# Block order at the end of an expert stage: the last up product ahead of the other block's down product

## The chip, the core and the metric

The kernel runs on one core of one Trainium2 chip. The metric is the device time of one execution in microseconds (us); the table below gives the median of three. The core's engines run side by side, each with its own list of instructions: TensorE (PE in the profile; its weight loads are PEld), VectorE (DVE), ScalarE (ACT), GpSimd (POOL) and SyncE (SP), which here only issues transfers. They wait for each other by semaphores.

## The reference, cut to what matters

The whole is a first block (norm, attention, a recurrent and a convolution branch, a mixture of experts) and a second block of two layers (a gated linear attention beside latent attention, then an FFT and gating mixer), on 1024 tokens of 1024 channels in fp32. The change lies where the experts end and the first layer of the second block begins:

```python
def run_block(args):                       # one expert, a block of its tokens
    xe, e = args
    return (jax.nn.silu(xe @ w_gate[e]) * (xe @ w_up[e])) @ w_down[e]
...
y = jnp.zeros((n_tok + 1, d), yb.dtype).at[slot_tok].add(yb * slot_gate[:, None])
...
# second block, layer 0: latents x and context ctx are normed and modulated, then projected
h_lat = modulate(x, shift, scale)
h_ctx = modulate(ctx, shift_c, scale_c)    # layer_norm(ctx) * (1 + scale_c) + shift_c
y_lat, y_ctx = even_mixer(h_lat, h_ctx, ...)
```

There are 32 experts; `w_gate` and `w_up` are 1024x512 for each, `w_down` 512x1024. The context has 256 rows and doesn't depend on the experts; the latents x do.

## The kernel before, in words

**Blocks of the expert stage.** The 32 experts are worked off in `NMB` = 26 blocks, numbered 0 to 25. Twenty are single experts with up to 128 tokens; six are pairs of two lightly used experts with up to 64 tokens each. Block 25 is a single one, block 24, ahead of it, is a pair. A block goes through: rows of its tokens gathered (POOL), turned on PE (`turn_tensor`), gate product (`product_tensor(p, n, 0, ...)`, "gu" n 0), up product ("gu" n 1), SiLU on ACT (L2162), hidden product silu(gate)*up on DVE ("hd", L2223), hidden rows turned on PE (`turn_hidden_tensor`, L2086) and copied (ACT L2173 or, for a pair, L2170, and DVE L2235), down product (`down_tensor`, two PSUM banks), output copies on ACT (`down_scalar`, L2181) and a scatter to `y2d` in memory by POOL (L2001).

**Weights.** Each of the three weights of a block comes as pieces of 1 MB: two of a single block, four of a pair. SP fetches them (L320) in the order of the list `turns`, into a ring of ten slots; a fetch waits until PE has done with what lay in its slot. The number before `_in` in a semaphore's name (`slot112_in`) is the slot. The weights of a single block are multiplied in three passes from a high and a low part: `WE.split_scalar` (ACT L385, two instructions for a piece) copies the rounded high part, `WE.split_vector` (DVE L394, two instructions) subtracts it. A product waits for the low part (`lo_done`). A pair's weights are used whole, without a split. ACT and DVE split three pieces ahead of the one in use (`ahead_scalar`, `ahead_vector`).

**Order.** The order on each engine is written out by hand: `experts_tensor`, `experts_scalar` and `experts_vector` loop over the blocks e: up product of e (with the rows of e+1 turned in its middle), gate product of e+1 (with the hidden rows of e turned in its middle), down product of e. In the last turn, without a block e+1, PE turns the hidden rows of block 25 and then the first half of the context (`nC.turn_tensor`, L527) ahead of block 25's down product.

**The context's norm.** ACT loads a table (L2471) and computes the reciprocal deviation (`stats_scalar`, L271 and L272); DVE makes the bias from it (`center_vector`, L491); ACT normalises one half of the rows (`norm_scalar`, L512), DVE the other (`norm_vector`, L500). Then PE turns them, and after block 25's output ACT (L553, L555) and DVE (L561, L574) scale and split them.

**What comes behind.** SP fetches two pieces of the next layer's weights: one once "gu" 25 1 is done, one once half of down 25 is done. POOL waits for "gu" 25 1, moves four tiles of x (`moves_pool`, L2385) and scatters block 25. When both last scatters have landed, SP loads `y2d` (L2378) and DVE combines the experts' outputs with x (`combine_vector`, L2394), from which the latents' norm and the next layer start.

## Time and profile before

| | us |
|---|---|
| median of 3 runs (lowest to highest) | 2316.39 (2315.34 to 2318.12) |
| the profiled execution | 2316.22 |
| its span, first to last instruction | 2314.4 |
| PE busy | 2163.4 (93%) |
| DVE busy | 1353.3 (58%) |
| ACT busy | 1030.2 (45%) |
| POOL busy | 365.9 (16%) |

The mean granted clock of TensorE was 0.979 of its full 2.4 GHz. Times in rows are counted from the span's start. The expert stage lies between about 600 and 1145 us, the place of the change between 1095 and 1160. In it the 16 DMA engines are busy over most of the time with the experts' weights, and PE nearly all of it; how the two end is what the rows below show.

### The profile page before, as it was taken

The page shows a single profiled execution, that of the slowest core. Times are in us where ns is not written, and L with a number is a line of the kernel's source. Part 1 is how long each engine was busy: PE and PEld are TensorE (multiplying, and loading weights), DVE is VectorE, ACT ScalarE, POOL GpSimd, SP SyncE. Part 2 cuts the span into 40 slices and gives each one's busy share as a digit, 9 for nine tenths or more (in the row PEclk, how much of TensorE's full clock was granted, in tenths as well). Part 3 has the DMA queues.
Part 4 walks back from the last instruction along what each step waited for, and adds up shares of the span by engine and source line. Part 5 has one row for each costly group of instructions (what it writes and reads, how often), then busy time and mean ns, then how long its engine had stood idle before and what let it go on. Part 6 is the DMA issues. An engine that isn't in the chain of part 4 may idle for free.

```text
span 2314.4 us, 26522 instructions
## 1 busy us (share of the span) xinstructions
PE 2163.4 (93%) x10595; PEld 1547.1 (67%) x10595; DVE 1353.3 (58%) x1733; ACT 1030.2 (45%) x1515; POOL 365.9 (16%) x263
## 2 busy tenths in 40 slices
PE   7999999898799998999879999988999999999998
PEld 6877755674676566565568777744555567788886
DVE  5787277456877457465572255566555556643385
ACT  4265366511666456455562234354544523402231
POOL 2000012000211011110200000013555623000014
PEclk9999999998999999999989999999999999999999
DMA  4111030217999999999661101030010031211041
GB/s 129 63 47 37 28 128 29 73 67 303 412 408 421 420 409 389 413 401 396 254 208 37 49 19 37 33 111 1 1 37 19 1 146 73 76 43 49 24 176 64
DMA packets 105889, 348.78 MB, mean 151 GB/s; under 512 B 21960, under 2 KB 54737, under 8 KB 79776
## 3 DMA queue, kind: packets, MB, share of 16 engines
q1 hardware_dynamic: 95040, 321.70, 36.3%
q0 software_dynamic: 9504, 21.08, 2.4%
q10 hardware_dynamic: 1216, 4.24, 0.5%
q8 instruction: 86, 1.41, 0.3%
q14 instruction: 43, 0.35, 0.0%
HBM read 323.21 MB, written 34.26 MB: 154 GB/s over the span
## 4 chain that ended last, share of the span: by engine, by line
PE 76%; DVE 9%; DMA 8%; ACT 5%; issue 2%; SPq 0%; POOL 0%; DVEq 0%; ACTq 0%; POOLq 0%
PE psm L236 72%; DMA mem<-in_exp_w_up_dram 4%; DVE small L3521 2%; DMA mem<-in_ada_w_dram 2%; DMA mem<-in_exp_w_gate_dram 1%; PE psm L1173 1%; ACT mem L1255 1%; DMA mem<-in_exp_w_down_dram 1%; PE psm L2040 1%; PE psm L527 1%; DVE r L350 1%; DVE r L394 1%; ACT r L385 1%; DVE mem L3226 0%; ACT mem L1209 0%
## 5 line engine op out<-in xcount | busy, mean ns | idle before, releaser
L236 PE MATMUL psm<-r,r 128*128 128x512 f32 (+3 forms) x6449 | 1544.9, 396 | 71.5 <-DVE r L2206 14.1
L236 PEld LDWEIGHTS psm<-r,r 128*128 128x128 f32 (+2 forms) x6449 | 1191.4, 190 | 408.4 <-issue 88.2
L236 PE MATMUL psm<-mem 128*64 128x512 f32 (+11 forms) x2870 | 464.0, 448 | 20.8 <-DMA mem<-in_ada_w_dram 10.7
L394 DVE TENSOR_TENSOR r<-mem,r 128x1024 fp32r<-128x1024 f32 x240 | 283.3, 1225 | 163.2 <-ACT r L385 160.4
L236 PEld LDWEIGHTS psm<-mem 128*64 128x64 f32 (+5 forms) x2870 | 205.3, 152 | 218.1 <-issue 160.7
L385 ACT ACTIVATE r<-mem 128x1024 fp32r<-128x1024 f32 x240 | 240.0, 1054 | 102.5 <-DMA mem<-in_exp_w_gate_dram 44.3
L3735 POOL TENSOR_TENSOR mem<-mem 128x1024 f32<-128x1024 f32 x63 | 152.5, 2421 | 161.7 <-ACT mem L3687 106.9
L3687 ACT ACTIVATE mem<-psm 128x512 f32<-128x512 f32 x160 | 94.4, 595 | 141.9 <-PE psm L236 135.3
L3521 DVE TENSOR_REDUCE small<-psm 128x1 f32<-128x1280 f32 x64 | 95.2, 1488 | 86.3 <-PE psm L236 86.3
L350 DVE TENSOR_TENSOR r<-mem,r 128x1024 fp32r<-128x1024 f32 (+2 forms) x72 | 76.9, 1111 | 79.8 <-ACT r L341 79.5
L1303 DVE TENSOR_TENSOR_SCAN mem<-mem,small 128x128 f32<-128x128 f32 (+7 forms) x64 | 83.7, 1356 | 24.3 <-POOL mem L1319 20.1
L271 ACT ACTIVATE small<-small 128x1 f32<-128x1 f32 (+2 forms) x34 | 10.0, 294 | 194.7 <-DVE small L431 123.9
L3876 POOL TENSOR_TENSOR mem<-mem 128x1024 f32<-128x1024 f32 (+1 forms) x15 | 35.7, 2379 | 375.5 <-ACT mem L3842 375.5
L236 PE MATMUL psm<-mem,cst 128*128 128x512 f32 (+4 forms) x222 | 79.4, 592 | 1.7 <-ACT mem L2685 1.0
L341 ACT ACTIVATE r<-mem 128x1024 fp32r<-128x1024 f32 (+2 forms) x72 | 63.2, 930 | 33.4 <-DMA mem<-in_w_in_dram 23.1
L1043 DVE SCALAR_TENSOR_TENSOR mem<-mem,small 128x1024 f32<-128x1024 f32 x60 | 76.9, 1281 | 1.3
L4058 ACT ACTIVATE mem<-psm 128x512 f32<-128x512 f32 x24 | 14.4, 598 | 138.3 <-PE psm L236 138.3
L2001 POOL DMA_INDIRECT y2d<-mem,small x26 | 27.1, 1042 | 304.1 <-ACT mem L2181 223.3
L1992 POOL DMA_INDIRECT mem<-h2d,small x26 | 31.0, 1193 | 209.5 <-DVE mem L2223 173.1
L574 DVE TENSOR_TENSOR r<-psm,r 128x256 fp32r<-128x256 f32 (+1 forms) x56 | 26.5, 492 | 47.8 <-ACT r L555 47.7
L1255 ACT ACTIVATE mem<-psm 128x1024 f32<-128x1024 f32 (+3 forms) x48 | 37.2, 811 | 38.0 <-PE psm L236 37.7
L1173 PE MATMUL psm<-cst,mem 128*128 128x128 f32 x288 | 42.5, 284 | 10.4 <-ACT mem L1209 9.6
(374 smaller groups left out, 1741.7 us busy)
## 6 DMA issues: line engine op xcount, KB each, us to landing
mem<-in_exp_w_gate_dram SPq DMA_DIRECT2D x64, 1024.0 KB, 17.4
mem<-in_exp_w_up_dram SPq DMA_DIRECT2D x64, 1024.0 KB, 17.4
mem<-in_exp_w_down_dram SPq DMA_DIRECT2D x64, 1024.0 KB, 17.8
mem<-in_ada_w_dram SPq DMA_DIRECT2D x32, 768.0 KB, 13.6
mem<-in_odd_w_in_dram SPq DMA_DIRECT2D x10, 1024.0 KB, 5.6
mem<-in_x_dram SPq DMA_DIRECT2D x16, 512.0 KB, 6.5
mem<-in_w_in_dram SPq DMA_DIRECT2D x8, 1024.0 KB, 5.3
mem<-y2d SPq DMA_DIRECT2D x8, 1024.0 KB, 7.0
```

The costliest lines, as they stand in the source:

```text
L236: return p.e.matmul(o, l, r, start=start, stop=stop, skip_group_check=True)
L341: p.e.activation(h, mem(self.raw(i), [R * n])[:, w * q:w * q + w], ACT.Copy).then_inc(*self.hi_done.up(i, q))
L350: p.e.tensor_tensor(l, mem(self.raw(i), [R * n])[:, w * q:w * q + w], h.bitcast(F32), SUB).then_inc(*self.lo_done.up(i, q))
L385: p.e.activation(h, mem(self.raw(i), [R * n])[:, w * q:w * q + w], ACT.Copy).then_inc(*self.hi_done.up(i, q))
L394: p.e.tensor_tensor(l, mem(self.raw(i), [R * n])[:, w * q:w * q + w], h.bitcast(F32), SUB).then_inc(*self.lo_done.up(i, q))
L1043: d = p.e.scalar_tensor_tensor(CA[:, j, :], UPC[:, j, i:i + 1024], tap(j, i), CA[:, j, :], MUL, ADD)
L1173: last = p.e.transpose(ps[:, o:o + 128], KP[s % 3][:, h, 128 * kb:128 * kb + 128], cst("ident"))
L1255: p.e.activation(KP[s % 3][:, :, 512 * c:512 * c + w], PSM[:, 2 * (k % 2):2 * (k % 2) + 2, 0:w], ACT.Sigmoid, scale=-1.0).then_inc(*at_act ...
L1303: p.e.tensor_tensor_scan(keep, keep, zero.broadcast_to([128, n]), 1.0, MUL, ADD).then_inc(*at_dve.up("left", s, h))
L3521: p.e.tensor_reduce(TOP[:, c:c + 1], PSM[:, 5:8, :].rearrange("p a b -> p (a b)")[:, 0:1280], AX, MAX).then_inc(*ml_dve.up("m", u, k))
L3687: p.e.activation(PT[t % 4][:, hd, :], PB.ps("s", t, hd), ACT.Exp, scale=SCALE).then_inc(*ml_act.up("e", t, hd))
L3735: p.e.tensor_tensor(sums, a, PT[t % 4], ADD).then_inc(*ml_pool.up(t))
```

## The change

In the list of fetches the up weights of block 25 come ahead of the down weights of block 24. On PE the whole up product of block 25 comes ahead of the down product of block 24, and block 25's hidden rows and the context are turned behind that. ACT and DVE follow: the splits of block 25's up weights go ahead, block 24's output copies stand behind the context's norm on ACT, and on DVE both steps of the context's norm stand ahead of the splits of block 25's down weights (before: behind them). No instruction is added or taken away.

```diff
         for n in range(NMB):
             turns += [(n, UW), (n + 1, GW), (n, DW)]
+        turns[-5:] = [(NMB - 1, GW), (NMB - 1, UW), (NMB - 2, DW), (NMB - 1, DW)]
...
         def experts_tensor(p):
...
-            for e in range(NMB):
-                product_tensor(p, e, 1, (lambda: turn_tensor(p, e + 1)) if e + 1 < NMB else None)
-                if e + 1 < NMB:
-                    product_tensor(p, e + 1, 0, lambda: turn_hidden_tensor(p, e))
-                else:
-                    turn_hidden_tensor(p, e)
-                    nC.turn_tensor(p, 0, CTX_ORDER[0:4], order=TURN_BANKS)
+            for e in range(NMB - 1):
+                product_tensor(p, e, 1, lambda: turn_tensor(p, e + 1))
+                product_tensor(p, e + 1, 0, lambda: turn_hidden_tensor(p, e))
+                if e == NMB - 2:
+                    product_tensor(p, NMB - 1, 1, None)
                 down_tensor(p, e)
+            turn_hidden_tensor(p, NMB - 1)
+            nC.turn_tensor(p, 0, CTX_ORDER[0:4], order=TURN_BANKS)
+            down_tensor(p, NMB - 1)
...
         def experts_scalar(p):
...
+                if e == NMB - 2:
+                    product_scalar(p, NMB - 1, 1, None)
                 for q in range(2):
                     ahead_scalar(p, units("exp_w_down", e, q))
-                    if q:
-                        down_scalar(p, e)
+                if e == NMB - 2:
+                    context_norm_scalar(p)
+                down_scalar(p, e)
+            turn_hidden_scalar(p, NMB - 1)
+            WV.split_scalar(p, 1)
+            down_scalar(p, NMB - 1)
...
         def experts_vector(p):
...
+                if e == NMB - 2:
+                    product_vector(p, NMB - 1, 1, None)
                 for q in range(2):
                     ahead_vector(p, units("exp_w_down", e, q))
+            turn_hidden_vector(p, NMB - 1)
...
         def product_vector(p, n, v, middle):
...
             if v == 1:
-                if n == NMB - 1:
-                    nC.center_vector(p)
                 p.wait_ge(*moe_pe.at("gu", n, 1, 1))
...
                 if n == NMB - 1:
+                    nC.center_vector(p)
                     nC.norm_vector(p)
```

Below is how the instructions stand in a row, with the kernel's line numbers; L2223 of before is L2224 after, L2235 is L2237, L2181 is L2184, L2170 is L2173, L2162 is L2165, L2173 is L2176.

DVE, from behind the splits of block 25's gate weights to the second step of the context's norm. `slot80_in` and `slot88_in` are the up weights of block 25 before, `slot112_in` and `slot104_in` after; `slot128_in` and `slot96_in` are its down weights in both. Before:

```order
L2223 TENSOR_TENSOR mem<-psm,mem 128x512 [waits moe_pe]
L394 TENSOR_TENSOR r_85<-mem,r_114 128x1024 [waits experts_hi,slot80_in]
L394 TENSOR_TENSOR r_87<-mem,r_115 128x1024 [waits experts_hi]
L394 TENSOR_TENSOR r_86<-mem,r_116 128x1024 [waits experts_hi,slot88_in]
L394 TENSOR_TENSOR r_88<-mem,r_117 128x1024 [waits experts_hi]
L394 TENSOR_TENSOR r_99<-mem,r_94 128x1024 [waits experts_hi,slot128_in]
L394 TENSOR_TENSOR r_101<-mem,r_96 128x1024 [waits experts_hi]
L394 TENSOR_TENSOR r_89<-mem,r_95 128x1024 [waits experts_hi,slot96_in]
L394 TENSOR_TENSOR r_91<-mem,r_97 128x1024 [waits experts_hi]
L491 SCALAR_TENSOR_TENSOR small<-small 128x2 [waits ctx_norm_act]
L2223 TENSOR_TENSOR mem<-psm,mem 128x512 [waits moe_act,moe_pe]
L500 TENSOR_SCALAR mem<-mem,small 128x1024 [waits ctx_norm_dve]
```

After:

```order
L394 TENSOR_TENSOR r_98<-mem,r_114 128x1024 [waits experts_hi,slot112_in]
L394 TENSOR_TENSOR r_100<-mem,r_115 128x1024 [waits experts_hi]
L2224 TENSOR_TENSOR mem<-psm,mem 128x512 [waits moe_pe]
L394 TENSOR_TENSOR r_90<-mem,r_116 128x1024 [waits experts_hi,slot104_in]
L394 TENSOR_TENSOR r_92<-mem,r_117 128x1024 [waits experts_hi]
L2224 TENSOR_TENSOR mem<-psm,mem 128x512 [waits moe_act,moe_pe]
L491 SCALAR_TENSOR_TENSOR small<-small 128x2 [waits ctx_norm_act]
L500 TENSOR_SCALAR mem<-mem,small 128x1024 [waits ctx_norm_dve]
L394 TENSOR_TENSOR r_99<-mem,r_94 128x1024 [waits experts_hi,slot128_in]
L394 TENSOR_TENSOR r_101<-mem,r_96 128x1024 [waits experts_hi]
L394 TENSOR_TENSOR r_89<-mem,r_95 128x1024 [waits experts_hi,slot96_in]
L394 TENSOR_TENSOR r_91<-mem,r_97 128x1024 [waits experts_hi]
```

The first up piece of block 25 (`r_98`, `r_100`) is now split ahead of block 24's hidden product (the first row that reads `psm` and `mem`). L491 and L500 have moved from behind the down weights' splits to ahead of them.

ACT, from the first down piece of block 25 (`slot128_in`) to the copy of block 25's hidden rows (L2173, after: L2176). Before:

```order
L385 ACTIVATE r_94<-mem 128x1024 [waits slot128_in]
L385 ACTIVATE r_96<-mem 128x1024
L2181 ACTIVATE mem<-psm 128x512 [waits moe_pe,y0_out]
L2181 ACTIVATE mem<-psm 128x512 [waits moe_pe]
L385 ACTIVATE r_95<-mem 128x1024 [waits slot96_in]
L385 ACTIVATE r_97<-mem 128x1024
L2471 ACT_TABLE_LOAD
L271 ACTIVATE small<-small 128x2 [waits ctx_norm_dve]
L272 ACTIVATE small<-small 128x2 [waits ctx_norm_act]
L512 ACTIVATE mem<-mem,small 128x1024 [waits ctx_norm_act,ctx_norm_dve]
L2173 ACTIVATE r_130<-psm 128x512 [waits moe_pe,ev_dve]
```

After:

```order
L385 ACTIVATE r_94<-mem 128x1024 [waits slot128_in]
L385 ACTIVATE r_96<-mem 128x1024
L385 ACTIVATE r_95<-mem 128x1024 [waits slot96_in]
L385 ACTIVATE r_97<-mem 128x1024
L2473 ACT_TABLE_LOAD
L271 ACTIVATE small<-small 128x2 [waits ctx_norm_dve]
L272 ACTIVATE small<-small 128x2 [waits ctx_norm_act]
L512 ACTIVATE mem<-mem,small 128x1024 [waits ctx_norm_act,ctx_norm_dve]
L2184 ACTIVATE mem<-psm 128x512 [waits moe_pe,y0_out,ev_dve]
L2184 ACTIVATE mem<-psm 128x512 [waits moe_pe]
L2176 ACTIVATE r_130<-psm 128x512 [waits moe_pe]
```

The two output copies of block 24 (`y0_out`) stood ahead of the last high part; now they stand behind L512, and both high parts of the down weights come first.

SP, the fetches of block 25's up weights and both blocks' down weights, up to the next layer's. Before:

```order
L320 DMA mem<-in_exp_w_down_dram 128x2048 [waits moe_pe]
L320 DMA mem<-in_exp_w_down_dram 128x2048
L320 DMA mem<-in_exp_w_down_dram 128x2048 [waits moe_pe] x2
L320 DMA mem<-in_exp_w_up_dram 128x2048 [waits moe_pe]
L320 DMA mem<-in_exp_w_up_dram 128x2048
L320 DMA mem<-in_exp_w_down_dram 128x2048 [waits moe_pe]
L320 DMA mem<-in_exp_w_down_dram 128x2048
L320 DMA mem<-in_even_w_in_dram 128x4x512 [waits moe_pe] x2
```

After:

```order
L320 DMA mem<-in_exp_w_up_dram 128x2048 [waits moe_pe]
L320 DMA mem<-in_exp_w_up_dram 128x2048
L320 DMA mem<-in_exp_w_down_dram 128x2048 [waits moe_pe] x3
L320 DMA mem<-in_exp_w_down_dram 128x2048
L320 DMA mem<-in_exp_w_down_dram 128x2048 [waits moe_pe]
L320 DMA mem<-in_exp_w_down_dram 128x2048
L320 DMA mem<-in_even_w_in_dram 128x4x512 [waits moe_pe] x2
```

The two up fetches go ahead of the four of block 24's down weights; the two of block 25's down weights stay last.

## Rows read from the trace of the kernel before

**Rows 1.** The page's first part: busy us, share of span, instructions of each engine.

```profile
PE 2163.4 (93%) x10595; PEld 1547.1 (67%) x10595; DVE 1353.3 (58%) x1733; ACT 1030.2 (45%) x1515; POOL 365.9 (16%) x263
```

**Rows 2.** Chain of waits, 1040 to 1180 us: start, duration in us, what.

```profile
1108.92 17.89 DMA mem<-in_exp_w_down_dram
...
1133.99 0.99 DVE small L491
1134.98 0.61 DVE mem L2223
...
1135.63 1.13 PE psm L2086 x4
...
1138.47 5.77 PE psm L236 x24
...
1158.92 1.30 DVE mem L2394
```

**Rows 3.** Timeline, 1112 to 1131 us: start, duration, engine, line, count, idle before.

```profile
1112.80 0.68 DVE L2223 TENSOR_TENSOR mem<-psm,mem 128x512 f32<-128x512 f32 x1
1113.56 0.73 PE L2086 MATMUL psm<-cst,mem 128*128 128x128 f32 x4
...
1116.96 7.09 PE L236 MATMUL psm<-mem 128*64 128x512 f32 x32
...
1121.91 2.00 ACT L385 ACTIVATE r<-mem 128x1024 fp32r<-128x1024 f32 x2 [4.25 <-DMA mem<-in_exp_w_up_dram]
...
1125.49 5.74 PE L236 MATMUL psm<-r,r 128*128 128x512 f32 x24 [1.44 <-DVE r L394]
```

**Rows 4.** Timeline, 1128 to 1139 us, the same columns.

```profile
1128.75 1.06 ACT L2181 ACTIVATE mem<-psm 128x512 f32<-128x512 f32 x2
1129.70 2.00 ACT L385 ACTIVATE r<-mem 128x1024 fp32r<-128x1024 f32 x2
1130.61 0.99 POOL L2001 DMA_INDIRECT y2d<-mem,small  x1 [27.55 <-ACT mem L2181]
1130.87 3.20 DVE L394 TENSOR_TENSOR r<-mem,r 128x1024 fp32r<-128x1024 f32 x2 [0.50 <-ACT r L385]
...
1131.57 5.82 POOL L2385 COPY mem<-mem 128x1024 f32<-128x1024 f32 x4
...
1133.02 0.30 ACT L271 ACTIVATE small<-small 128x2 f32<-128x2 f32 x1
...
1136.56 1.91 PE L527 MATMUL psm<-cst,mem 128*128 128x128 f32 x8
...
1137.49 0.69 DVE L2235 TENSOR_TENSOR r<-psm,r 128x512 fp32r<-128x512 f32 x1 [0.99 <-ACT r L2173]
```

**Rows 5.** DMA view of two single issues: start on SP, then size, us to landing.

```profile
1095.00 0.33 SPq L320 DMA_DIRECT2D mem<-in_exp_w_down_dram  x1
mem<-in_exp_w_down_dram SPq DMA_DIRECT2D x1, 1024.0 KB, 17.0
...
1109.35 0.38 SPq L320 DMA_DIRECT2D mem<-in_exp_w_down_dram  x1
mem<-in_exp_w_down_dram SPq DMA_DIRECT2D x1, 1024.0 KB, 19.9
```

**Rows 6.** Timeline elsewhere: four splits on DVE; a norm of the latents.

```profile
1074.56 4.81 DVE L394 TENSOR_TENSOR r<-mem,r 128x1024 fp32r<-128x1024 f32 x4
...
1167.17 0.30 ACT L271 ACTIVATE small<-small 128x2 f32<-128x2 f32 x1 [4.68 <-DVE small L431]
...
1167.73 0.16 DVE L491 SCALAR_TENSOR_TENSOR small<-small 128x2 f32<-128x2 f32 x1 [0.60 <-ACT small L272]
...
1167.93 0.81 DVE L500 TENSOR_SCALAR mem<-mem,small 128x1024 f32<-128x1024 f32 x1
```

**Rows 7.** Twelve matmuls twice; a stretch's busy times, then PEclk, DMA share, GB/s.

```profile
1059.96 4.60 PE L236 MATMUL psm<-r,r 128*128 128x512 f32 x12 [2.58 <-DVE r L394]
...
1084.12 3.00 PE L236 MATMUL psm<-r,r 128*128 128x512 f32 x12
...
1136.00:1137.00 1.00, 1.00 (x7) 0.99 (x6) 0.49 (x1) 0.40 (x2) 1.00 (x1) 0.50 0.05 18
```

More of the change, by code:

```diff
@@ L2123, in experts_scalar @@
             product_scalar(p, 0, 0, None)
-            for e in range(NMB):
-                product_scalar(p, e, 1, (lambda: turn_scalar(p, e + 1)) if e + 1 < NMB else None)
-                if e + 1 < NMB:
-                    product_scalar(p, e + 1, 0, lambda: turn_hidden_scalar(p, e))
-                else:
-                    context_norm_scalar(p)
-                    turn_hidden_scalar(p, e)
-                    WV.split_scalar(p, 1)
+            for e in range(NMB - 1):
+                product_scalar(p, e, 1, lambda: turn_scalar(p, e + 1))
+                product_scalar(p, e + 1, 0, lambda: turn_hidden_scalar(p, e))
+                if e == NMB - 2:
+                    product_scalar(p, NMB - 1, 1, None)
                 for q in range(2):
                     ahead_scalar(p, units("exp_w_down", e, q))
-                    if q:
-                        down_scalar(p, e)
+                if e == NMB - 2:
[4 more added lines that the diff above has]
+            down_scalar(p, NMB - 1)
         def turn_scalar(p, n):
@@ L2186, in experts_vector @@
             product_vector(p, 0, 0, None)
-            for e in range(NMB):
+            for e in range(NMB - 1):
                 if e == NMB - 6:
                     context_stats_vector(p)
-                product_vector(p, e, 1, (lambda: turn_vector(p, e + 1)) if e + 1 < NMB else None)
-                if e + 1 < NMB:
-                    product_vector(p, e + 1, 0, lambda: turn_hidden_vector(p, e))
-                else:
-                    turn_hidden_vector(p, e)
+                product_vector(p, e, 1, lambda: turn_vector(p, e + 1))
+                product_vector(p, e + 1, 0, lambda: turn_hidden_vector(p, e))
+                if e == NMB - 2:
+                    product_vector(p, NMB - 1, 1, None)
                 for q in range(2):
                     ahead_vector(p, units("exp_w_down", e, q))
+            turn_hidden_vector(p, NMB - 1)
         def turn_vector(p, n):
```

## The prediction, made before the changed kernel ran

> **What bounds the kernel now.** I read first the page's busy shares [rows 1]: TensorE (PE) is busy 93% of the span, so a change can only pay where PE waits. The change touches one place, the hand-over from the last two expert blocks to the next layer, so I went from there to the chain of waits [rows 2]. The reader should see that near 1130 us it leaves PE: the last expert weights land, VectorE (DVE) splits them, computes the context norm's L491, then the hidden product L2223 of block 25, and only then PE turns that block's hidden rows, turns the context and starts block 25's down product at 1138.47. From there it goes through block 25's output, its scatter and the splitting of the context to the combine, L2394 at 1158.92. So **the start of block 25's down product sets when the next layer starts**; I take what happens to it as what happens to the time. The timelines [rows 3, 4] give each engine's durations, the DMA issues [rows 5] the landings.
>
> PE ends block 25's up product at 1125.49+5.74=1131.23 [rows 3] and next works at 1135.63 [rows 2]: 4.4 us idle. Those are what a reader would hope to fill with block 24's down product, 7.09 us [rows 3].
>
> **The change, part by part.**
>
> *The weights.* Eight pieces of 1 MB (four of block 24's down weights, two each of block 25's up and down weights) are asked for in the same number of slots at the same moments; only which piece is which changes. The first is asked for at 1095.00 and lands 17.0 us later, at 1112.0; the last of block 25's down pieces is asked for at 1109.35 and lands 19.9 us later, at 1129.25 [rows 5]. The one before that landed at 1108.92+17.89=1126.81 [rows 2]: a piece in some 2.45 us. Block 25's up pieces then land at 1112.0 and about 1114.5 instead of 1121.9 [rows 3] and 1124.4. The down pieces of block 25 keep their places: **1129.25 stays**. Cost: 0.
>
> *The earlier up product.* A landed piece is usable when both halves are split: 1121.91 to PE's start at 1125.49 is 3.58 us [rows 3]. So the first up piece is ready at 1112.0+3.55=1115.55. On DVE that split now stands ahead of block 24's hidden product, which stood at 1112.80 [rows 3]; it comes at 1115.5, and the hidden turn of block 24 on PE, which came 0.76 us behind it (1113.56), at 1116.3. PE loses 2.7 us there. Then it runs gate 25, second half (3.4 us from the turn to the down product: 1116.96-1113.56), up 25 from 1119.7 to 1125.4, and down 24, 7.09 us, to 1132.5. All of down 24's pieces have landed by 1124.4. Block 25's hidden product is on DVE at 1125.5, and PE turns it at 1132.5 without a wait. So the edit does on PE what it says: the 4.4 us are filled. If PE alone decided, the down product would follow the turn as soon as the hidden rows are split: 0.75 us of turn, about 1.4 us of ScalarE (ACT) and DVE, hence at 1134.7, 3.8 us earlier than 1138.47. The 2.7 us lost ahead are covered, since ACT and DVE wait for the landing at 1129.25 in any case.
>
> *The context's norm on DVE.* Here the time turns. In the new order DVE has L491 and L500 ahead of the four splits of block 25's down weights; before, the splits came first. L491 waits for ACT's L271 and L272, and ACT has these behind its own copies of both down pieces. From the last landing: ACT's copy and the table load, 1133.02-1129.70=3.32 us [rows 4], give 1132.6; from L271 to L491 it is 1167.73-1167.17=0.56 where DVE is free [rows 6], hence 1133.15; L500 follows 0.20 later and takes 0.81 [rows 6], hence 1134.2. DVE stands idle from about 1126.2 to 1133.15, with the first down piece there since 1126.8. Then come the four splits, 4.81 us [rows 6], hence 1139.0; the low half of block 25's hidden rows, 0.69 us (at 1137.49 in [rows 4]), hence 1139.7. That is +1.2 us against 1138.47.
>
> *Block 24's output and GpSimd (POOL).* On ACT the output copies of block 24, 1.06 us, and the hidden copy of block 25 now stand behind L512, which starts with L500 at 1133.4 and takes 1.2 us. The output copies end near 1135.7; POOL's scatter comes 0.80 us behind (1130.61 against 1128.75+1.06), and its four moves start 0.96 behind that [rows 4]: near 1137.4. Before, they started at 1131.57. They used to lie over a pair of splits and made it 3.20 us long [rows 4], where four take 4.81, or 2.40 a pair: 0.8 us lost. Now they meet the last of the four splits. The cost lies between 0 and a whole copy, 5.82/4=1.45; I take the 0.8 of the row, since about as much of the pair is exposed. DVE ends at 1140.4, **the down product starts at 1140.5, +2.0 us**.
> The Trainium skill ("SBUF — State Buffer", Who interferes with whom) says that a DVE instruction with two SBUF inputs and a GpSimd one that reads SBUF lock each other out for a whole instruction. The row of 3.20 us agrees that they block each other, and shows an average price below a whole copy; by a full lock on each of the last two splits it would be 2.9 us instead of 0.8.
>
> The moves end near 1144 at most, and block 25's output comes at about 1147.5, so its scatter doesn't wait for them. Block 25's hidden copy on ACT, done by 1136.3, is hidden too. The first even weight is asked for at the up product's end, some 5.8 us earlier, and so lands before it is wanted: no gain, since its split stands behind block 25's.
>
> *PE's clock.* PE now idles just ahead of the down product: after the eight context turns, which end about 1136, until 1140.5, some 4.5 us. Rows show what such a pause does: after 2.58 us of idling twelve matmuls took 4.60 us where twelve usually take 3.00, and behind today's 4.4 us the granted clock was 0.50 (1.2 of 2.4 GHz) [rows 7], but there the turns bore it: the eight at 1136.56 took 1.91 us, and the 24 of the down product 5.77 to 5.79, against 5.74 in [rows 3]. In the new order the pause stands ahead of these 24. Price: between 0 and 1.6 us; I take 1.4, near the upper end, as the pause is longer than the 2.58 us that cost 1.6.
>
> *Sum.* 0 (weights) + 1.2 (norm ahead of splits) + 0.8 (moves) + 1.4 (clock) = +3.4 us on the end of down 25. What follows (output, scatter, context splits, combine) hangs on that end by the chain, and shifts with it. The profiled execution took 2316.22 us, 2314.4 of it the span, and 0.17 us below the median of the runs; so 2316.2+3.4=**2319.6 us**, +0.15%.
>
> **The rivals.**
> *The clock is spared, or the moves miss the splits.* For it: after 1.44 us of idling at 1125.49 the 24 matmuls took their usual 5.74 us [rows 3], and the turns in between count as work. Against it: the pause is three times that. Sum +1.2 to +2.0: 2317.4 to 2318.2.
> *The clock stays low for the whole down product (slower).* Place: PE, from 1140.5. The turns between two pauses are thin work, so the low clock may last beyond the first twelve matmuls. Price: all 24 at 4.60/12 give 9.2 instead of 5.74, +3.5 in place of 1.4: 2321.7. It decides from the point where the clock comes back only after the eighteenth matmul (+2.4 in place of 1.4 gives 2320.6, still within the bound; the last six go beyond).
> *A full lock (slower).* The moves block two splits for a whole copy each, +2.9 in place of 0.8: 2321.7. Against it: the row of the pair, 3.20, shows 0.8. This is the case in which the rule of the Trainium skill ("SBUF — State Buffer") holds at its hardest.
> *The promised gain.* The down product starts at 1134.7, -3.8: 2312.4. It needs DVE to split the down weights before the norm; its written order says no, and only much earlier landings, which the same requests don't give, would undo that.
> *The change doesn't do what it says* is excluded for PE's order, but in effect it is my main case: the stall is moved from PE's wait on block 25's hidden product to its wait on the splits.
>
> **How the numbers follow.** Chances: main case (2318.5 to 2320.9) 0.50; spared 0.22; clock low throughout 0.13; full lock 0.08; gain 0.07. The range leaves out the gain and the tails: 2317.0 to 2322.0. A measurement of this kernel can tell about 0.2%, 4.6 us, from no change. Slower by more are the two slower rivals: 0.21. Faster by more is only a gain beyond 3.8 us: 0.02. The rest, main case, spared and most of the gain, is within: 0.77.
>
> **What would show it.** In the new profile: block 24's hidden turn on PE near 1116 with some 2.7 us of waiting for L2224 (L2223's new line); the up product of block 25 then runs on to down 24 without a pause; the last down piece's copy on ACT still at 1129.3; L491 at 1133.2 with DVE idle for some 7 us ahead; the four splits behind it, the last of them longer; down 25 at 1140.5, with 7 us or more for its 24 matmuls; and the combine some 3.4 us later than 1158.92. I'd be wrong if the last piece landed much earlier, if the combine hung on something else than block 25's output, or if down 25 started before 1138.5.

## The result and the profile after

The changed kernel is slower by a little more than I had forecast. Eight runs gave a median of 2324.05 us (2320.14 to 2325.09), against 2316.55 us (2315.16 to 2320.26) for eight of the kernel before: a ratio of 1.0029, with a 95% interval of 1.0020 to 1.0039. I had written 2319.6 us, 2317.0 to 2322.0. The sign of the sum was right; the time lies above the range, and the outcome with the highest chance, within 0.2%, did not hold in this measurement. Measured twice more with the experiments below, the same kernel took 2320.75 and 2321.69 us, ratios 1.0018 (1.0009 to 1.0027) and 1.0017 (1.0008 to 1.0026), which is where the forecast had it. So there are two things to explain: the 3 to 4 us that repeat, and the other 4 of the first 7.5 us.

First the place of the change. The timeline of the changed kernel there (columns: start us, duration us, engine, line, operation, operands, count, and in brackets the idle time before and what ended it):

```profile
1112.71 2.99 PE L236 MATMUL psm<-r,r 128*128 128x512 f32 x12 [1.68 <-DVE r L2209]
...
1117.52 0.68 DVE L2224 TENSOR_TENSOR mem<-psm,mem 128x512 f32<-128x512 f32 x1
...
1118.26 0.75 PE L2088 MATMUL psm<-cst,mem 128*128 128x128 f32 x4 [2.56 <-DVE mem L2224]
1118.76 8.42 PE L236 MATMUL psm<-r,r 128*128 128x512 f32 x36
...
1127.11 7.09 PE L236 MATMUL psm<-mem 128*64 128x512 f32 x32
...
1131.45 2.00 ACT L385 ACTIVATE r<-mem 128x1024 fp32r<-128x1024 f32 x2 [0.55 <-DMA mem<-in_exp_w_down_dram]
...
1134.13 0.75 PE L2088 MATMUL psm<-cst,mem 128*128 128x128 f32 x4
...
1135.33 0.16 DVE L491 SCALAR_TENSOR_TENSOR small<-small 128x2 f32<-128x2 f32 x1 [7.41 <-ACT small L272]
...
1136.26 5.50 DVE L394 TENSOR_TENSOR r<-mem,r 128x1024 fp32r<-128x1024 f32 x4
1136.67 1.06 ACT L2184 ACTIVATE mem<-psm 128x512 f32<-128x512 f32 x2
...
1136.91 1.94 PE L527 MATMUL psm<-cst,mem 128*128 128x128 f32 x8 [2.03 <-ACT mem L512]
...
1138.53 0.99 POOL L2002 DMA_INDIRECT y2d<-mem,small  x1 [33.32 <-ACT r L2176]
1139.49 7.12 POOL L2387 COPY mem<-mem 128x1024 f32<-128x1024 f32 x4
...
1141.68 0.68 DVE L2237 TENSOR_TENSOR r<-psm,r 128x512 fp32r<-128x512 f32 x1
...
1142.62 7.61 PE L236 MATMUL psm<-r,r 128*128 128x512 f32 x23 [3.76 <-DVE r L2237]
```

The reader should see the whole forecast in these rows. PE waits 2.56 us for block 24's hidden product (L2224), runs the second half of block 25's gate product and its up product without a pause (12 and 24 matmuls) and block 24's down product behind them; the 4.4 us of idling of [rows 2] are filled. DVE is idle for 7.41 us ahead of L491, and the four splits (L394) stand behind it. They take 5.50 us where four take 4.81 [rows 6], as GpSimd's moves start at 1139.49. PE turns the hidden rows at 1134.13, waits 2.03 us for the context's norm (L512), turns the context, and its down product begins at 1142.62, after another 3.76 us of idling. (The last row counts 23 matmuls, since the window asked for ends inside the product; the chain below has all 24.)

One instruction bears the whole loss of the splits (shortest, median and longest of the four in ns, start of the first and the last):

```profile
L394 DVE TENSOR_TENSOR r<-mem,r x4: 1218/1238/2051, 1136.3 to 1139.7; 128x1024 fp32r<-128x1024 f32 x4
```

Only the last split overlaps a move. It starts at 1139.7, behind the first move's start at 1139.49, and takes 2.05 us where the others take 1.22 to 1.26.

The chain of waits (start, duration, what) gives the landing, the down product of all 24 matmuls and the combine, to be held against [rows 2]:

```profile
1111.50 19.93 DMA mem<-in_exp_w_down_dram
...
1142.62 7.85 PE psm L236 x24
...
1165.15 1.29 DVE mem L2396
```

I count all times in the place from the start of block 25's gate product, g: 1110.72 in the kernel before, 1112.71 here. The down product starts at g+29.91 (before: 1138.43-1110.72, g+27.71), so 2.2 us later, where I had +2.0. It lasts 7.85 us and not 5.77. The combine starts at g+52.44 instead of g+48.20, 4.2 us later.

These 4.2 are less than half of the 8.9 us between the two spans (2323.3 and 2314.4). Another 1112.71-1110.72=2.0 us were there before block 25's gate product began, where only the order of the last fetches differs, and 2.7 arose after the combine had begun, where no instruction has moved.

The clock tells what the down product's 7.85 us are. Busy times by stretch; the columns are PE, PEld, DVE, ACT, POOL, then the granted clock of PE, the DMA share and GB/s:

```profile
1137.00:1139.00 2.00, 1.85 (x8) 1.45 (x8) 2.00 (x3) 2.00 (x4) 0.47 (x1) 0.50 0.00 0
1140.00:1142.00 2.00, 0.00 (x0) 0.00 (x0) 2.00 (x2) 0.11 (x1) 2.00 (x2) 0.50 0.34 131
1142.00:1144.00 2.00, 1.39 (x3) 1.16 (x4) 2.00 (x3) 0.00 (x0) 2.00 (x2) 0.50 0.00 0
1146.00:1148.00 2.00, 2.00 (x7) 1.58 (x7) 0.00 (x0) 0.00 (x0) 0.61 (x1) 0.69 0.00 0
```

The clock is at its lower level (0.50, 1.2 of 2.4 GHz) through the turns and the pause, and comes back only within 1146 to 1148, between 4 and 5 us after the down product has begun. It was already low when the context was turned, behind the wait of 2.03 us.

### The profile page after: what moved, and what is told of

The parts are those of the page before. It is cut to its first block, busy times and chain, and to the rows that moved or that the text cites. A ratio compares the mean times of both kernels' runs of the same rounds, so it can differ in the third digit from the quotient of the medians.

```text
span 2323.3 us, 26521 instructions
## 1 busy us (share of the span) xinstructions
PE 2169.9 (93%) x10595; PEld 1552.3 (67%) x10595; DVE 1353.7 (58%) x1733; ACT 1030.2 (44%) x1515; POOL 367.7 (16%) x263
## 4 chain that ended last, share of the span: by engine, by line
PE 73%; DVE 11%; DMA 9%; ACT 5%; issue 2%; SPq 0%; POOL 0%; DVEq 0%; ACTq 0%; POOLq 0%
PE psm L236 70%; DMA mem<-in_exp_w_up_dram 4%; DVE small L3523 2%; DMA mem<-in_ada_w_dram 2%; DMA mem<-in_exp_w_gate_dram 1%; DVE mem L1043 1%; PE psm L1173 1%; DMA mem<-in_exp_w_down_dram 1%; DVE r L350 1%; ACT mem L1255 1%; PE psm L2042 1%; PE psm L527 1%; DVE r L394 1%; DMA mem<-in_odd_w_out_dram 1%; ACT r L385 1%
## 5 line engine op out<-in xcount | busy, mean ns | idle before, releaser
L394 DVE TENSOR_TENSOR r<-mem,r 128x1024 fp32r<-128x1024 f32 x240 | 283.2, 1224 | 150.4 <-ACT r L385 147.6
L3689 ACT ACTIVATE mem<-psm 128x512 f32<-128x512 f32 x160 | 94.4, 596 | 141.7 <-PE psm L236 135.0
L350 DVE TENSOR_TENSOR r<-mem,r 128x1024 fp32r<-128x1024 f32 (+2 forms) x72 | 78.0, 1126 | 79.5 <-ACT r L341 79.3
L4060 ACT ACTIVATE mem<-psm 128x512 f32<-128x512 f32 x24 | 14.3, 598 | 137.9 <-PE psm L236 137.9
L2184 ACT ACTIVATE mem<-psm 128x512 f32<-128x512 f32 x52 | 30.1, 591 | 52.2 <-PE psm L236 52.2
```

What stands on the lines that cost most here:

```text
L350: p.e.tensor_tensor(l, mem(self.raw(i), [R * n])[:, w * q:w * q + w], h.bitcast(F32), SUB).then_inc(*self.lo_done.up(i, q))
L394: p.e.tensor_tensor(l, mem(self.raw(i), [R * n])[:, w * q:w * q + w], h.bitcast(F32), SUB).then_inc(*self.lo_done.up(i, q))
L3689: p.e.activation(PT[t % 4][:, hd, :], PB.ps("s", t, hd), ACT.Exp, scale=SCALE).then_inc(*ml_act.up("e", t, hd))
```

## The experiments

The table gives for each traced kernel where its events lie, worked out from its timeline as above: the start of block 25's down product and of the combine, counted from g; how long the down product took; and the span less the stretch from g to the combine, which is everything outside the place.

| kernel | down 25 starts | takes | combine starts | rest of the span |
|---|---|---|---|---|
| before | 27.7 | 5.8 | 48.2 | 2266.2 |
| before_again | 27.8 | 7.2 | 49.6 | 2270.6 |
| after | 29.9 | 7.9 | 52.4 | 2270.9 |
| after_again | 29.8 | 7.5 | 52.0 | 2272.2 |
| after_third | 29.9 | 7.9 | 52.5 | 2266.1 |
| splits_first | 26.4 | 6.3 | 47.4 | 2265.7 |
| norm_early | 24.0 | 5.7 | 44.4 | 2263.0 |
| norm_early_again | 25.6 | 5.7 | 46.0 | 2265.4 |
| moves_first | 29.1 | 8.5 | 52.3 | 2266.5 |
| filler | 30.9 | 6.1 | 51.7 | 2271.2 |
| filler_short | 29.1 | 5.7 | 49.5 | 2267.2 |
| before_norm | 26.9 | 7.2 | 48.8 | 2269.0 |
| best | 23.1 | 7.4 | 45.1 | 2269.5 |

### The two kernels again

> The kernel before, once more, as a control. The changed kernel took 7.5 us more by the medians, and its trace shows 4.1 us of that between block 24's gate product and the combine. The other 3.4 us lie elsewhere, in stretches in which PE's granted clock was 0.50 in one trace and 1.00 in the other. Theory A (low-clock stretches elsewhere move from program to program or run to run, and the change has no part in their size): this run's trace has stretches of low clock at other places than the first trace of before, and its parts outside 1095 to 1165 us differ by a microsecond or two. Theory B (they are a lasting effect of the change): this run's low stretches lie where they lay, and its time is 2316.5 within 1.5 us. Ratio expected by both: 1.000.

> The changed kernel, once more. Both theories: the down product of block 25 starts 2.0 us later than in the kernel before, counted from the first matmul of block 25's gate product. Theory A: the low-clock stretches lie elsewhere than in its first trace, the down product of block 25 takes between 5.8 and 8 us (7.85 in the first trace), and the ratio lies between 1.001 and 1.003. Theory B: the same stretches, the same 7.85 us, and a ratio of 1.003.

> The changed kernel a third time. Its first median lay 7.5 us above that of the kernel before, its second 3.5 us. If the time outside the place of the change varies with the stretches of low clock from run to run and the change adds 3 to 4 us, the ratio lies at 1.0015 again, between 1.0005 and 1.0025, and the trace shows 51.9 to 52.5 us from block 25's gate product to the combine. If the first result was the true size, the ratio is 1.003.

The medians and ratios: before_again 2318.13 us, 1.0005 (0.9996 to 1.0015); after_again 2320.75, 1.0018; after_third 2321.69, 1.0017. The kernel before, timed beside these runs, spread from 2315.06 to 2323.05. From before_again, after_again and after_third, in this order, the down product and the combine:

```profile
1140.89 7.19 PE L236 MATMUL psm<-r,r 128*128 128x512 f32 x24
...
1162.77 2.61 DVE L2394 SCALAR_TENSOR_TENSOR mem<-mem,small 128x1024 f32<-128x1024 f32 x2 [1.30 <-issue]
```

```profile
1141.78 7.45 PE L236 MATMUL psm<-r,r 128*128 128x512 f32 x24 [4.59 <-DVE r L2237]
...
1163.93 2.61 DVE L2396 SCALAR_TENSOR_TENSOR mem<-mem,small 128x1024 f32<-128x1024 f32 x2 [1.30 <-issue]
```

```profile
1141.56 7.90 PE L236 MATMUL psm<-r,r 128*128 128x512 f32 x24 [3.80 <-DVE r L2237]
...
1164.17 2.61 DVE L2396 SCALAR_TENSOR_TENSOR mem<-mem,small 128x1024 f32<-128x1024 f32 x2 [1.30 <-issue]
```

Two things follow. The kernel before, unchanged, took 7.19 us for its down product in its second trace and 5.77 in its first, since the low clock reached past the turns into it; so a part of this cost is in both kernels. And outside the place the same kernel differs by 4.4 us from trace to trace (before: 2266.2 and 2270.6), the changed one by 6.1 (2266.1 to 2272.2). The values of the two kernels lie among each other, so no effect of the change is seen there. Theory A stands, as far as traces show it. Within the place the means are 48.9 us of two traces before and 52.3 of three after: **the change costs about 3.4 us there**. With so few traces that is a mean of pairs between 2.4 and 4.3 us.

The changed kernel's second trace also tells which of PE's two waits matters. There PE came late and waited only 0.35 us ahead of the context's turns:

```profile
1136.07 1.12 PE L527 MATMUL psm<-cst,mem 128*128 128x128 f32 x8 [0.35 <-ACT mem L512]
```

The turns took 1.12 us and not 1.94, so the clock was still high, and the down product behind the pause of 4.59 us took 7.45 us all the same. That pause alone is enough.

### One part undone: the splits ahead of the norm on VectorE

```diff
 def product_vector ...
                 if n == NMB - 1:
-                    nC.center_vector(p)
-                    nC.norm_vector(p)
...
 def experts_vector ...
                 for q in range(2):
                     ahead_vector(p, units("exp_w_down", e, q))
+            nC.center_vector(p)
+            nC.norm_vector(p)
             turn_hidden_vector(p, NMB - 1)
```

> The changed kernel with VectorE's two steps of the context's norm (L491, L500) put back behind the four splits of block 25's down weights; ScalarE's order stays. My theory: the splits end 3.5 us behind the last landing, L491 and L500 follow at once, the hidden rows' low half comes behind L500, and the down product starts some 3 us earlier than in the changed kernel (4.81 us of splits no longer stand behind L500; ScalarE's output copies and hidden copy then set it, L512 and three copies behind L491), 1 us or so earlier than in the kernel before. Time about 2316.5-1=2315.5, up to 2318 if the clock is low there. Rival (ScalarE's order, not VectorE's, is what costs): less than 1 us of change against the changed kernel, above 2322.

Its median is 2316.05 us, ratio 0.9994 (0.9985 to 1.0003). Its timeline:

```profile
1113.10 2.97 PE L236 MATMUL psm<-r,r 128*128 128x512 f32 x12 [1.81 <-DVE r L2211]
...
1130.42 4.85 DVE L394 TENSOR_TENSOR r<-mem,r 128x1024 fp32r<-128x1024 f32 x4 [2.13 <-ACT r L385]
...
1135.63 0.16 DVE L491 SCALAR_TENSOR_TENSOR small<-small 128x2 f32<-128x2 f32 x1 [0.36 <-ACT small L272]
...
1139.51 6.31 PE L236 MATMUL psm<-r,r 128*128 128x512 f32 x24 [0.43 <-DVE r L2236]
```

The splits end at 1135.27, ahead of L491, and cost nothing any more. The down product starts 3.5 us earlier than in the changed kernel and 1.3 earlier than in the kernel before. By the time of the runs this kernel can't be told from the kernel before. So the order of two steps on VectorE is what turned the change from about even to a loss. It acts in three ways at once here: the splits no longer wait for the norm, the moves no longer meet them (4.85 us instead of 5.50), and PE's pause ahead of the down product shrinks to 0.43 us (6.31 us instead of 7.85).

### The norm early on ScalarE

```diff
 def experts_scalar ...
                 if e == NMB - 2:
                     product_scalar(p, NMB - 1, 1, None)
+                    context_norm_scalar(p)
                 for q in range(2):
                     ahead_scalar(p, units("exp_w_down", e, q))
-                if e == NMB - 2:
-                    context_norm_scalar(p)
                 down_scalar(p, e)
```

> The changed kernel with one call moved: ScalarE does the context's norm (table, L271, L272, L512) ahead of its copies of block 25's down weights instead of behind them; VectorE's order stays. My theory (VectorE's splits of the last down weights wait behind L491, which waits for ScalarE, which waits for the last landing): L491 runs as soon as block 25's hidden product is done, some 7 us earlier, the splits follow the landings, and the down product starts some 5.8 us earlier than in the changed kernel and 3.8 us earlier than in the kernel before; with the clock no longer low there some 2 us more. Time about 2316.5-3.8=2312.7 us, 2311 to 2315. Rival (the down product waits for something else, block 24's output copies or the landing itself): the start moves by less than 2 us, and the time stays above 2321.

> norm_early once more, to see how far its gain repeats. Expected: the down product starts 24.0 us behind block 25's first gate matmul and the combine comes at 44.4 us, against 48.2 to 49.6 in the kernel before; ratio 0.998, between 0.997 and 0.999.

Medians 2312.05 and 2312.99 us, ratios 0.9982 (0.9972 to 0.9991) and 0.9980 (0.9969 to 0.9990): faster than both kernels. The timeline of the first:

```profile
1110.43 3.00 PE L236 MATMUL psm<-r,r 128*128 128x512 f32 x12 [1.68 <-DVE r L2208]
...
1125.75 0.15 DVE L491 SCALAR_TENSOR_TENSOR small<-small 128x2 f32<-128x2 f32 x1
...
1128.23 4.63 DVE L394 TENSOR_TENSOR r<-mem,r 128x1024 fp32r<-128x1024 f32 x4 [1.47 <-ACT r L385]
...
1132.64 1.05 PE L527 MATMUL psm<-cst,mem 128*128 128x128 f32 x8
...
1134.42 5.69 PE L236 MATMUL psm<-r,r 128*128 128x512 f32 x24 [0.73 <-DVE r L2236]
```

L491 now runs right behind block 25's hidden product, the splits follow the landings, and PE pauses only 0.73 us ahead of the down product, which then runs at full clock. The start, g+24.0, is 3.7 us earlier than before; I had worked out 3.8 for a down product that waits for PE alone. In its second trace it came at g+25.6 and the combine at g+46.0, and my 24.0 and 44.4 were missed: there the 36 matmuls of gate and up product took 10.05 us instead of 8.45, since the low clock (0.50 from 1119 to 1121 us) fell on them behind the wait of 2.71 us for block 24's hidden product. So what is lost there is covered in the changed kernel (in its second trace the 36 took 10.02 us, and the down product started at g+29.8 as in the others), where the path waits for the landing and the norm, but not in this one.

### Is it the norm's place alone?

```diff
 # on the kernel before
 def experts_scalar ...
                 if e + 1 < NMB:
                     product_scalar(p, e + 1, 0, lambda: turn_hidden_scalar(p, e))
+                    if e == NMB - 2:
+                        context_norm_scalar(p)
                 else:
-                    context_norm_scalar(p)
                     turn_hidden_scalar(p, e)
...
 # and on VectorE center_vector and norm_vector likewise, behind product_vector(p, e + 1, 0, ...)
```

> The kernel before with the context's norm alone moved: ScalarE and VectorE do it after block 25's SiLU, ahead of that block's up product. The order of weights and products is that of before. It tells whether norm_early's gain comes from the norm's place alone. My theory (the early up product gives most of it, the norm only has to be out of the way): block 25's hidden product no longer waits for L491 (0.99 us) but still for the splits of the last down weights, so the down product starts about 1 us earlier than in the kernel before; time 1 us below it, ratio 0.9995. Rival (the norm's place is all): the down product starts 3 to 4 us earlier, ratio 0.998 as in norm_early.

Median 2316.89 us, ratio 0.9995 (0.9985 to 1.0005). Timeline:

```profile
1120.22 0.16 DVE L491 SCALAR_TENSOR_TENSOR small<-small 128x2 f32<-128x2 f32 x1 [6.05 <-ACT small L272]
...
1134.81 0.68 DVE L2225 TENSOR_TENSOR mem<-psm,mem 128x512 f32<-128x512 f32 x1
...
1138.29 7.22 PE L236 MATMUL psm<-r,r 128*128 128x512 f32 x24
```

The down product starts at g+26.9, 0.8 us earlier than before, 1 us expected. So of the 3.7 us of norm_early's first trace some 0.8 are the norm's place; the rest needs the early up product. By these two traces the change's idea is worth about 3 us at the start of the down product, and its norm took them and more. The time of before_norm can't be told from that of the kernel before.

### The moves, alone

```diff
 def experts_pool ...
-            scatter(p, NMB - 2)
             p.wait_ge(*moe_pe.at("gu", NMB - 1, 1, 1))
             moves_pool(p, (2, 3, 4, 5))
+            scatter(p, NMB - 2)
```

> The changed kernel with GpSimd's four moves (L2387) ahead of its scatter of block 24, so that they run from the end of block 25's up product, while VectorE waits for ScalarE, and not over the last splits. My term for the moves was 0.8 us; the trace of the changed kernel shows 5.50 us for four splits that take 4.63 to 4.81 where no move runs. Expected: the moves take about 4 us, the four splits 4.7 us, the down product starts 0.8 us earlier than in the changed kernel (1.2 us later than in the kernel before), and its time lies 1 us below the changed kernel's. Rival (the splits are longer for another reason, such as ScalarE's copies beside them): they stay at 5.5 us.

```profile
1125.79 3.99 POOL L2387 COPY mem<-mem 128x1024 f32<-128x1024 f32 x4 [22.03 <-PE psm L236]
...
1134.76 4.67 DVE L394 TENSOR_TENSOR r<-mem,r 128x1024 fp32r<-128x1024 f32 x4
...
1140.28 8.48 PE L236 MATMUL psm<-r,r 128*128 128x512 f32 x24 [3.33 <-DVE r L2237]
```

The splits take 4.67 us instead of 5.50, and the down product starts 0.8 us earlier, as expected. The time doesn't follow: 2323.34 us, ratio 1.0017 (1.0008 to 1.0027). In this trace the down product took 8.48 us, the longest of all, and the combine came no earlier than in the changed kernel. The expected gain of 1 us in time wasn't seen.

### The pause and the clock

```diff
 def experts_tensor ...
             turn_hidden_tensor(p, NMB - 1)
+            filler_tensor(p, 3)          # filler_short: 2
             nC.turn_tensor(p, 0, CTX_ORDER[0:4], order=TURN_BANKS)
+            filler_tensor(p, 5)          # filler_short: 3
             down_tensor(p, NMB - 1)
+
+        def filler_tensor(p, k):
+            for _ in range(k):
+                mm(p, banks[7][:, :], cst("ident"), CS[:, 0:512], True, True)
```

> The changed kernel with eight matmuls of 128x128 by 128x512 into an unused PSUM bank, three ahead of the context's turns and five behind them, in PE's pause ahead of block 25's down product; their result is used nowhere. My theory (the pause lowers the clock, and the down product pays for it): the start stays where it is in the changed kernel, the granted clock is 1.00 through the down product, and its 24 matmuls take 5.7 to 5.8 us instead of 7.45 to 7.85. Time some 2 us below the changed kernel's, about 2319. Rival (the low clock comes whatever PE does): 7 us or more, and no gain.

> The changed kernel with five filling matmuls in PE's pause, two ahead of the context's turns and three behind, instead of eight, which overran the pause by 1.0 us. Expected: the down product starts where it does in the changed kernel, 29.8 to 29.9 us behind block 25's first gate matmul, and takes 5.7 to 6.1 us instead of 7.45 to 7.85, so the combine comes 1.5 to 2 us earlier than in the changed kernel. Rival (the filling delays the turns, or the clock falls in the gaps that are left): a combine at 52 us as in the changed kernel.

The long filling gave 2320.13 us, ratio 1.0007 (0.9998 to 1.0016); the short one 2320.18, 1.0010 (1.0001 to 1.0018). The changed kernel's later intervals, 1.0008 to 1.0027 together, overlap both, so the gain is shown by the traces and not by the times. The short one's timeline:

```profile
1109.85 3.00 PE L236 MATMUL psm<-r,r 128*128 128x512 f32 x12 [1.81 <-DVE r L2215]
...
1133.46 4.62 DVE L394 TENSOR_TENSOR r<-mem,r 128x1024 fp32r<-128x1024 f32 x4
...
1135.74 2.07 POOL L2002 DMA_INDIRECT y2d<-mem,small  x1 [33.53 <-ACT r L2182]
1137.78 3.17 POOL L2393 COPY mem<-mem 128x1024 f32<-128x1024 f32 x2
...
1138.94 5.72 PE L236 MATMUL psm<-r,r 128*128 128x512 f32 x24 [1.12 <-DVE r L2243]
...
1159.37 2.61 DVE L2402 SCALAR_TENSOR_TENSOR mem<-mem,small 128x1024 f32<-128x1024 f32 x2 [1.30 <-issue]
```

With PE kept busy the 24 matmuls take 5.72 us instead of 7.45 to 7.90: the pause is what lengthens them. The combine comes at 49.5, 2.8 us earlier than the three traces' mean, of which 2.0 are the clock. The other 0.8 come from an earlier start (29.1, where I had expected 29.8 to 29.9): GpSimd's issue of the scatter took 2.07 us here instead of 0.99, so the moves began later, at 1137.78, and met only the end of the last split. With the long filling the issue took 2.07 us and the splits 4.62 us too. Why the issue took longer I don't know. The long filling overran the pause, its down product starting at g+30.9 and not at the expected g+29.8, and so gave part back. Its 24 matmuls are at the full clock too (1.00); their 6.05 us begin while the last filling still runs.

### Two more moves on top of norm_early

```diff
 # on norm_early; experts_scalar: block 24's output copies behind block 25's hidden copy
-                down_scalar(p, e)
+                if e < NMB - 2:
+                    down_scalar(p, e)
             turn_hidden_scalar(p, NMB - 1)
+            down_scalar(p, NMB - 2)
...
 # product_vector, block 24: the split of the first up piece behind the hidden product
+            late = v == 1 and n == NMB - 2
             for q in range(2):
-                ahead_vector(p, units(("exp_w_gate", "exp_w_up")[v], n, q))
+                if not (late and q):
+                    ahead_vector(p, units(("exp_w_gate", "exp_w_up")[v], n, q))
...
                 PB.frees(("gu", n, 1), moe_dve.at("hd", n))
+                if late:
+                    ahead_vector(p, units("exp_w_up", n, 1))
```

> norm_early with two more moves of order. VectorE computes block 24's hidden product ahead of the split of block 25's first up piece, so that PE's new wait of 2.7 us for it goes; ScalarE copies block 25's hidden rows ahead of block 24's outputs. Expected: PE is some 2.6 us ahead at block 25's hidden turn, and the down product then waits for the splits of the last down weights, which end 3.6 us behind the last landing: its start comes 1 to 1.5 us earlier than in norm_early, not 2.6. Time about 1 us below norm_early's. Rival (the last landing doesn't bind, PE does): 2.6 us below it.

Median 2314.22 us, ratio 0.9980 (0.9971 to 0.9989), the same as norm_early's and not 1 us better.

```profile
1128.91 4.75 DVE L394 TENSOR_TENSOR r<-mem,r 128x1024 fp32r<-128x1024 f32 x4 [4.13 <-ACT r L385]
...
1134.52 7.35 PE L236 MATMUL psm<-r,r 128*128 128x512 f32 x24 [2.80 <-DVE r L2242]
```

The down product starts 0.9 us earlier than in norm_early, bound by the last landing as expected (I had 1 to 1.5). But PE, now ahead, pauses 2.80 us instead of 0.73, and the down product takes 7.35 us instead of 5.69: in this trace the clock took back more than the order gave.

## Why the prediction was wrong, point by point

- **The weights.** Held. The last piece landed at 1111.50+19.93=1131.43, g+18.7; before, at 1129.25, g+18.5.
- **The earlier up product.** Held: 2.56 us lost where I had 2.7, the 4.4 us filled, the hidden rows turned early.
- **The norm ahead of the splits.** Held, shown by splits_first and norm_early. L491 comes at g+22.6; I had 1133.15, g+22.4. The sum's +1.2 is there: with the moves out of the way the down product starts at g+29.1, 1.4 us later than before. The 0.2 over the sum's term are PE's own start, 0.26 us behind the end of L2237 (1141.68+0.68 to 1142.62), which the sum left out.
- **The moves.** The size held: 5.50 us for the four splits, 4.67 without the moves, a difference of 0.83 for my 0.8. The 2.9 us of the rival "full lock" didn't come, but not because the engines share. The last split alone took 2.05 us instead of 1.22, and the moves beside VectorE's work took up to 2.03 us each instead of 1.0; the figures fit each waiting out the instruction that it finds running. The rival was wrong in letting this fall on two splits; it fell on one, as in the pair of [rows 4] (1.23 and 2.06 us). The Trainium skill ("SBUF — State Buffer", Who interferes with whom) says that a VectorE instruction with two SBUF inputs contends with a GpSimd one that reads SBUF, and that this is an exclusive lock. These rows agree, since the loss falls on whole instructions. That my average of the pair gave the right 0.8 was in part luck.
- **The clock.** The mechanism held, shown by the filling. The size was right as a difference of means (7.75 us of three traces less 6.5 of two is 1.3, for 1.4), but not as a pair: between the first two traces it was 2.1. I had taken 5.77 us as what the kernel before always pays. Its second trace has 7.19, and before_norm, with its wait of 3.44 us ahead of the same turns, 7.22. So the size rests on few traces, and the 1.3 may be too much.
- **The sum.** +3.4 us to the combine forecast, 3.4 found between the means of the traces, 3.5 and 3.6 us between the medians of the two later measurements. The mechanism is right; that the figures meet to 0.1 us is luck, with pairs of traces between 2.4 and 4.3.
- **The step that failed** is the one from the sum to the time and its range: "What follows ... hangs on that end by the chain, and shifts with it", with a range made of the change's own terms. Outside the place one kernel's traces differ by 4 to 6 us, and I gave this nothing, without a reason. In the first two traces 4.7 of the 8.9 us were of that kind. The forecast also hung on one time of the kernel before, 2316.2 us; its later medians are 2317.25 to 2318.93. By my estimate a range that takes such differences in would have reached from about 2314 to 2325, and the chance of slower by over 0.2%, a bound only 1.2 us above my forecast, should have been nearer to 0.4 than to 0.21.

What stays open is why the first measurement gave 7.5 us. Its eight runs of the changed kernel lie close together at 2324, some 3 us above the later 23 runs' medians but within their spread (2317.87 to 2326.06), and by the means only 1.7 us above (2323.7 and 2322.0); the kernel before was at its lowest there. So chance may be enough, but that isn't shown.

The traces show in part what differs outside the place. Busy times of the first two traces behind the start of the combine, in the columns of above:

```profile
1158.92:2314.40 1155.48, 1094.34 (x5333) 797.76 (x5331) 623.93 (x871) 439.70 (x697) 250.93 (x125) 0.98 0.18 60
1165.15:2323.30 1158.15, 1097.78 (x5334) 800.79 (x5332) 623.98 (x871) 439.75 (x697) 250.91 (x125) 0.98 0.18 60
```

The stretch is 2.7 us longer, and PE is busy 3.4 us longer with the same work, while VectorE, ScalarE and GpSimd keep their times within 0.1 us. That fits the clock, and so do the runs: 28 later ones of the kernel before with a mean granted clock of 0.975 to 0.977 took 2319.8 us on average, 41 with 0.979 to 0.981 took 2317.0. Ahead of g the clock explains little: there the stretch is 2.0 us longer with only 0.2 us more of PE (1030.15 against 1029.92), so most of those 2.0 us are waits, and for what isn't shown. They aren't the change's: g lies 2.4 us apart in the two traces of the kernel before (1110.72 and 1113.14), and at 1110.43 in norm_early, which has the new order of fetches.

## What to carry to other kernels

When a product is pulled ahead to fill an engine's idle time, look at what the other engines now do in the new order: here VectorE sat idle for 7 us, some 5 of them with work ready behind a small step that waited for ScalarE, and putting that step first on ScalarE, where nothing was due, turned +3.4 us in the place into about -3.7 (-5 by the medians). A pause in front of dense matmuls can cost more than itself; that it costs less in front of light work (the turns) is suggested by one trace of three here and not shown. And a range needs, beside the change's own terms, how far two traces of the unchanged kernel lie apart.

## What the runs showed of the hardware

- The granted clock behind a pause is not the same from run to run for one kernel: the same 24 matmuls of the kernel before, behind the same wait of 4.4 us and the same turns, took 5.77 us in one trace and 7.19 in another. The same 36 matmuls of gate and up product took 8.42 us behind a wait of 2.56 us in the changed kernel's first trace and 10.02 behind 2.58 us in its second.
- Against the 5.74 us of [rows 3] the down product took between 1.7 and 2.7 us more behind pauses of 3.3 to 4.6 us, 1.6 behind one of 2.80, and nothing behind one of 0.73. It took 0.6 more behind one of 0.43 in splits_first, where the clock was already low in the turns, behind 1.96 us of waiting.
- Useless matmuls in the pause kept the granted clock at 1.00, and the 24 matmuls behind them took 5.72 us.
- GpSimd copies of 128x1024 and VectorE's splits (two inputs in SBUF, the core's on-chip memory) lengthen each other. A copy took 1.0 to 1.1 us unhindered and up to 2.03 us beside a split; a split took 1.22 us alone and 2.05 beside a copy. Four copies took 3.99 us with VectorE all but idle, and 5.36 to 7.12 us where the two took turns.
- They don't always take turns. In norm_early VectorE's first split of the next layer's weights (L350) started 0.02 us ahead of the first copy (1134.53) and took 5.11 us, as long as all four copies and itself, while the copies ran at their full speed, 4.01 us for the four. In splits_first the same split took 5.30 us beside 4.02 us of copies:

```profile
L350 DVE TENSOR_TENSOR r<-mem,r x2: 1210/3162/5114, 1134.5 to 1139.5; 128x1024 fp32r<-128x1024 f32 x2
...
1134.53 4.01 POOL L2386 COPY mem<-mem 128x1024 f32<-128x1024 f32 x4
```

It cost nothing there, since VectorE's next instruction waited for ScalarE 0.93 us longer anyway. On a path that others wait for, it would cost some 4 us by my estimate (5.11 less 1.21). What decides between the two ways isn't shown.
- A small VectorE instruction suffers as well: L491, on 128x2 elements, took 0.99 us beside a copy in the kernel before and 0.16 us where none ran.
